# Folding the turn stage of a hybrid encoder block into its projection loop

## The chip, the cores and the metric

The kernel runs on one NeuronCore of one Trainium2 chip. The metric is the device time of one execution in microseconds (us), here the median of three runs. Profiles come from one further execution that the hardware profiler recorded.

## The reference: what is computed

Two groups of 256 tokens (512 in all, model width 1024) go through one encoder layer with the same weights. Cut to what matters here:

```
n1 = rmsnorm(h, W['norm_mix'][i])
proj = n1 @ W['w_in'][i]
xbc = silu(centred_depthwise_conv(xbc, conv_w) + conv_b)      # ssd: x, B, C
qkv = silu(centred_depthwise_conv(qkv, conv_w))               # gdn: q, k, v
q, k, v = l2norm(heads(q)), l2norm(heads(k)), heads(v)
```

After that come a bidirectional state-space scan over x, B and C (SSD), a bidirectional gated delta rule over queries, keys and values (GDN), a merge through an output projection, an expert layer (PEER) and a gated per-layer embedding. `l2norm` divides each head's 128 channels by the root of their sum of squares at each token. The scans want x, the values and also the keys by token and not by channel, so those are transposed.

## The kernel before, in words

The program is a row of stages with a barrier of all engines between them (`end_stage`). The change touches the first two. Five engines run side by side, each in the order of its own instruction list, and wait for one another by semaphores: TensorE (`pe`, in the profile PE), VectorE (`dve`), ScalarE (`act`), GpSimd (`pool`) and SyncE (`sp`), which issues the loads.

**`project_stage`** (L270 to L471). `NormT` (L201) squares the four token tiles of 128 tokens (ScalarE, L216), makes one root for all four (L229, L219, L231), scales them (VectorE, L233), transposes them into eight PSUM banks (TensorE, L245) and copies each bank out as a high part (ScalarE, L223) and a low part (VectorE, L237): `n_high` and `n_low`. A float32 product is made of three products of such parts (`products`, L172; L178, L179, L180). Then comes the small product with 64 columns (decays and gates), its transposes (L347), and a loop over 40 channel tiles: five trips of eight tiles (`Fori`). The order of the tiles in memory is x (8), B (4), C (4), queries (8), keys (8), values (8), by `CH_X` to `CH_V` (L475). For a tile TensorE runs 24 matmuls of 128x128 on 128x512. ScalarE takes the bank out with the centre tap (L405), VectorE adds three taps (L464), ScalarE applies silu (L400). Weights come in chunks of two tiles: SyncE loads 1 MB (L313), ScalarE makes the high part (L411), GpSimd the low part (L334). Behind the loop stand four small decay matmuls (L364), their exponential (L421) and a negation (L471).

**`turn_stage`** (L478 to L576) begins after the barrier. ScalarE squares the 16 tiles of queries and keys (L511). TensorE sums each over its 128 channels by a plain float32 matmul whose stationary operand is 128x16 (L529): tile k lands in row k of one bank. ScalarE takes the roots (L513), VectorE inverts them (L566), and high and low parts of the 16 rows are made (L517, L569). TensorE turns x and the values (L540), then spreads each inverse norm over 128 partitions with a 16x128 selector (L552, L553), VectorE multiplies (L575), and TensorE turns the keys. 24 groups of four transposes fill banks 4 to 7; ScalarE empties one half of them (L521), VectorE the other (L563).

**`ssd_stage`** (L644) begins after another barrier, with ScalarE at L675. It and all later stages keep their code, except that they find the tiles of B and C at other places of `channels`.

## Time and profile before

| what | us |
|---|---|
| median of 3 runs | 2458.65 (2453.87 to 2460.51) |
| the profiled execution | 2451.77 |
| its span, first to last instruction | 2450.0 |
| PE busy in the span | 2301.3 |
| DVE busy | 1529.1 |
| POOL busy | 1228.5 |
| ACT busy | 863.1 |

Busy time of PE is the union of its matmuls from start to modelled end. A matmul ends about 0.16 us after the next could start, so the pace of a row of matmuls is read from their starts. PEld is the load of the stationary operand, which overlaps PE. PEclk is TensorE's granted clock as a share of its full 2.4 GHz. L numbers are lines of the kernel before.

### The profile page before, as it was taken

The numbers are of one execution on the slowest core, as the hardware profiler recorded it, in microseconds if no ns is written. First come the engines' busy times: TensorE is split into PE (matmuls) and PEld (weight loads), VectorE is DVE, ScalarE is ACT, GpSimd is POOL, SyncE is SP. The second block draws the span as 40 slices with busy tenths as digits, with TensorE's granted clock in tenths as the row PEclk, the third lists the DMA queues.
The fourth block names the chain that finished last, engine by engine and source line by source line (L and its number), as shares of the span: only waits on it lengthen the run. The fifth ranks groups of instructions, "written<-read, shape, count | busy, mean of one in ns | idle before, by whom it ended". The sixth has DMA issues, their size and how long they took to land. (4 is left out here: it accounts for less than half of the span.)

```text
span 2450.0 us, 31801 instructions
## 1 busy us (share of the span) xinstructions
PE 2301.3 (94%) x10852; PEld 1890.1 (77%) x10852; DVE 1529.1 (62%) x3496; ACT 863.1 (35%) x1271; POOL 1228.5 (50%) x982
## 2 busy tenths in 40 slices
PE   7999889899979997989999999999989999999977
PEld 5888577788878886777888888888878888888865
DVE  5444488676764342119887887885238888888833
ACT  5443433334434331314333333333233233323322
POOL 3343086566544432413556656665647765555411
PEclk9999899999999998999999999999999999999989
DMA  4221011133344231314444444446449999999720
GB/s 144 101 88 66 0 57 39 41 120 128 129 145 173 93 117 41 128 36 144 141 142 141 141 141 142 142 142 210 142 146 405 378 377 361 356 349 349 299 103 35
DMA packets 158980, 393.98 MB, mean 161 GB/s; under 512 B 26304, under 2 KB 91968, under 8 KB 148160
## 3 DMA queue, kind: packets, MB, share of 16 engines
q1 hardware_dynamic: 124096, 325.79, 38.4%
q0 software_dynamic: 34816, 67.41, 7.4%
q8 instruction: 27, 0.44, 0.1%
q14 instruction: 41, 0.34, 0.0%
HBM read 327.92 MB, written 65.21 MB: 160 GB/s over the span
## 5 line engine op out<-in xcount | busy, mean ns | idle before, releaser
L1662 POOL DMA_INDIRECT g_dense<-up_gates_summed_sb,up_gate_at_sb x384 | 416.6, 1085 | 324.1 <-issue 230.3
L178 PE MATMUL ps<-n_high_sb,up_u_high_sb 128*128 128x512 f32 x1024 | 404.9, 395 | 7.9 <-DVE up_u_low_sb L1530 7.9
L179 PE MATMUL ps<-n_low_sb,up_u_high_sb 128*128 128x512 f32 x1024 | 404.5, 395 | 0.0
L180 PE MATMUL ps<-n_high_sb,up_u_low_sb 128*128 128x512 f32 x1024 | 404.5, 395 | 0.0
L1863 PE MATMUL ps<-down_v_high_sb,down_w_high_sb 128*128 128x512 f32 x768 | 299.6, 390 | 7.6 <-DVE down_w_low_sb L1813 7.6
L1864 PE MATMUL ps<-down_v_low_sb,down_w_high_sb 128*128 128x512 f32 x768 | 299.5, 390 | 0.0
L1865 PE MATMUL ps<-down_v_high_sb,down_w_low_sb 128*128 128x512 f32 x768 | 299.3, 390 | 0.0
L1530 DVE TENSOR_TENSOR up_u_low_sb<-up_u_sb,up_u_high_sb 128x1024 fp32r<-128x1024 f32 x128 | 156.5, 1223 | 173.7 <-ACT up_u_high_sb L1683 173.2
L1771 ACT ACTIVATE down_v_high_sb<-down_v_sb 128x1024 fp32r<-128x1024 f32 x128 | 134.3, 1049 | 322.8 <-PE ps L1865 289.5
L178 PEld LDWEIGHTS ps<-n_high_sb,up_u_high_sb 128*128 128x128 f32 x1024 | 193.3, 189 | 53.2 <-DVE up_u_low_sb L1530 8.1
L180 PEld LDWEIGHTS ps<-n_high_sb,up_u_low_sb 128*128 128x128 f32 x1024 | 193.3, 189 | 45.2
L179 PEld LDWEIGHTS ps<-n_low_sb,up_u_high_sb 128*128 128x128 f32 x1024 | 193.4, 189 | 45.0
L1696 ACT ACTIVATE up_gelu_sb<-ps 128x512 f32<-128x512 f32 x128 | 76.5, 597 | 418.3 <-PE ps L180 418.2
L1790 POOL DMA_INDIRECT expert_rows_sb<-expert_v,chosen_expert_sb x128 | 160.7, 1255 | 116.4 <-DVE h_sb L1829 63.3
L1811 DVE TENSOR_TENSOR down_v_low_sb<-down_v_sb,down_v_high_sb 128x1024 fp32r<-128x1024 f32 x128 | 156.4, 1222 | 71.2 <-ACT down_v_high_sb L1771 71.1
L1782 POOL DMA_INDIRECT down_picked_gelu_sb<-a_dense,chosen_gelu_at_sb x128 | 147.5, 1152 | 69.0 <-issue 69.0
L1863 PEld LDWEIGHTS ps<-down_v_high_sb,down_w_high_sb 128*128 128x128 f32 x768 | 144.6, 188 | 38.1 <-DVE down_v_low_sb L1811 8.1
L1171 POOL TENSOR_TENSOR merge_low_sb<-merge_slots_sb,merge_high_sb 128x2048 fp32r<-128x2048 f32 x19 | 88.2, 4640 | 167.8 <-ACT merge_high_sb L1159 167.8
L464 DVE SCALAR_TENSOR_TENSOR channels_sb<-ps,column_params_sb,channels_sb 128x510 f32 (+1 forms) x120 | 89.7, 748 | 126.5 <-ACT channels_sb L405 112.1
L1864 PEld LDWEIGHTS ps<-down_v_low_sb,down_w_high_sb 128*128 128x128 f32 x768 | 144.6, 188 | 30.1
L1865 PEld LDWEIGHTS ps<-down_v_high_sb,down_w_low_sb 128*128 128x128 f32 x768 | 144.6, 188 | 30.0
L334 POOL TENSOR_TENSOR w_low_sb<-w_slots_sb,w_high_sb 128x2048 fp32r<-128x2048 f32 x20 | 92.4, 4621 | 129.1 <-ACT w_high_sb L411 123.2
(324 smaller groups left out, 4729.7 us busy)
## 6 DMA issues: line engine op xcount, KB each, us to landing
up_u_sb<-expert_u SPq DMA_DIRECT2D x128, 512.0 KB, 3.8
down_v_sb<-expert_v SPq DMA_DIRECT2D x32, 2048.0 KB, 11.9
a_dense<-up_gelu_sb SPq DMA_DIRECT2D x128, 256.0 KB, 2.2
g_dense<-nought_sb SPq DMA_DIRECT2D x8, 3072.0 KB, 10.4
down_gelu_sb<-a_dense SPq DMA_DIRECT2D x32, 768.0 KB, 4.8
down_gates_sb<-g_dense SPq DMA_DIRECT2D x32, 768.0 KB, 6.5
w_slots_sb<-w_conv SPq DMA_DIRECT2D x20, 1024.0 KB, 4.9
query_slots_sb<-peer_query SPq DMA_DIRECT2D x8, 1024.0 KB, 5.3
```

The costliest lines, as they stand in the source:

```text
L178: pe.matmul(out, ah, bh, start=k == 0, stop=False)
L179: pe.matmul(out, ah, bl, start=False, stop=False)
L180: last = pe.matmul(out, al, bh, start=False, stop=k == n - 1)
L1530: dve.tensor_tensor(ul[:, n, :, :], u[:, n, :, :], bits32(uh[:, n, :, :]), ALU.subtract).then_inc(low, 1)
L1662: pool.indirect_dma_start(cells, at, summed[:, tt, k:k + 1], None).then_inc(stored[tt], 16)
L1771: act.activation(vh[b][:, j, :], v[:, b, j, :], ACT.Copy).then_inc(v_high, 1)
L1782: pool.indirect_dma_start(picked[:, u, k:k + 1], None, gelus, at).then_inc(gelu_in[n % 2], 16)
L1790: pool.indirect_dma_start(m.rows[:, s, :], None, experts, at).then_inc(row_in[s], 16)
L1811: dve.tensor_tensor(vl[b][:, j, :], v[:, b, j, :], bits32(vh[b][:, j, :]), ALU.subtract).then_inc(v_low, 1)
L1863: pe.matmul(m.ps[:, q, :], wh[:, b, j, t], vh[b][:, j, c], start=start, stop=False)
L1864: pe.matmul(m.ps[:, q, :], wh[:, b, j, t], vl[b][:, j, c], start=False, stop=False)
L1865: return pe.matmul(m.ps[:, q, :], wl[:, b, j, t], vh[b][:, j, c], start=False, stop=stop)
```

## The change

`turn_stage` is gone as a stage. Its work stands inside `project_stage`, whose loop over 40 tiles is written out. The tiles now come in the order x, keys, values, queries, B, C, and `laid` maps this to the unchanged order of the weights. Each tile product is followed on TensorE by what is due behind that tile: a sum over the squares of the tile two before (16 in all), a spread of one or two inverse norms (16 in all, of two matmuls each), and a group of four transposes (24 in all). Sums are kept for eight heads at a time, with a 128x128 stationary operand cut from `strip`, and the selectors of the spreads are 128x128 too. Tile products use banks 0 to 3 and no longer 0 to 7. The decay matmuls stand behind tile 19, the small product behind tile 1 and its transposes behind tile 2.

The norm becomes `NormTiles`: each token tile is squared, rooted, scaled and transposed by itself. SyncE loads only the first square (the identity) and the columns' parameters between the tokens; the other constants come later; the first weight chunk is loaded and split in two halves.

The core of the diff:

```diff
-    for stage in (project_stage, turn_stage, ssd_stage, gdn_stage, merge_stage):
+    for stage in (project_stage, ssd_stage, gdn_stage, merge_stage):
...
+CH_X, CH_K, CH_V, CH_Q, CH_B, CH_C = 0, 8, 16, 24, 32, 36
...
-    norm = NormT(nc, m, m.region(AT_CH, AT_WORK), "mix_norm", COL_MIX)
+    norm = NormTiles(nc, m, m.region(AT_CH, AT_WORK), "mix_norm", COL_MIX)
...
+    BANKS = 4
+    NH = GDN_H
+    SQUARED = 2
+    LAG = 2
+    FIRST = (CH_K, CH_Q)
+    NORMS_AT = [c + NH + LAG for c in FIRST]
+    SPREAD_AT = [t + 3 for t in NORMS_AT]
+    DECAYS_AT = NORMS_AT[0] + 1
...
+    def turns_behind(t):
+
+        for n, first in enumerate((CH_X + 6, CH_V + 6, CH_V + 14)):
+            if first <= t < first + 8:
+                return [8 * n + t - first]
+        return []
...
+    def spreads_behind(t):
+        if SPREAD_AT[0] <= t < SPREAD_AT[0] + NH:
+            return [t - SPREAD_AT[0]]
+        k = 2 * (t - SPREAD_AT[1])
+        return [NH + n for n in (k, k + 1) if 0 <= n < NH] if t < N_CONV else [NH + n for n in range(max(k, 0), NH)]
...
+            for t in range(N_CONV):
+                tile_product(t, first if t == 0 else lambda k: None)
+                if t == 1:
+                    pe.wait_ge(small_low, 1)
+                    products(pe, m.ps[0:64, 6, :], [(wsh[:, k, :], wsl[:, k, :]) for k in range(KT)],
+                             [(m.nh[:, k, :], m.nl[:, k, :]) for k in range(KT)]).then_inc(small_prod, 1)
...
+                k = head_of(t - LAG)
+                if k is not None:
...
+                    pe.wait_ge(squared, k + 1)
+                    j = k % NH
+                    pe.matmul(m.ps[:, 4, :], strip[:, NH - 1 - j:NH - 1 - j + P], s2[:, k % SQUARED, :], start=j == 0,
+                              stop=j == NH - 1).then_inc(summed, 1)
...
+                spreads(t)
+                for g in turns_behind(t):
+                    base, _, half, tt = turn(g)
+                    if base == CH_K:
+                        pe.wait_ge(scaled, 4 * half + 4)
+                    else:
+                        pe.wait_ge(active, base + 4 * half + 4)
+                    if g >= 2:
+                        pe.wait_ge(copied[g % 2], g // 2)
+                    for a in range(4):
+                        last = pe.transpose(m.ps[:, 6 + g % 2, a * P:(a + 1) * P],
+                                            m.ch[:, base + half * 4 + a, tt * P:(tt + 1) * P], sq(m, "eye"))
+                    last.then_inc(turned, 1)
+            spreads(N_CONV)
```

The turn stage before, on TensorE, from the last rows of the projection on (L364 the decays, L529 the sums, L540 the transposes, L552 and L553 the spreads):

```order
L180 MATMUL ps<-n_high_sb,w_low_sb 128x512
L350 REGISTER_ALU
L350 COMPARE_AND_BRANCH
L364 MATMUL ps<-decay_sb,squares_sb 128x64 x4
L299 UNCONDITIONAL_BRANCH
L523 UNCONDITIONAL_BRANCH
L529 MATMUL ps<-squares_of_sb,column_strip_sb 16x512 x16
L540 MATMUL ps<-squares_sb,channels_sb 128x128 x64
L552 MATMUL ps<-norms_high_sb,row_selectors_sb 128x512
L553 MATMUL ps<-norms_low_sb,row_selectors_sb 128x512
```

Sums, transposes and spreads stand there in blocks of their own, and no tile product is left to run between them.

TensorE in the changed kernel, behind the product of tile 26 (L513 a sum, L488 a spread, L532 a group of transposes):

```order
L180 MATMUL ps<-n_high_sb,w_low_sb 128x512
L513 MATMUL ps<-squares_of_sb,column_strip_sb 128x512
L488 MATMUL ps<-norms_high_sb,row_selectors_sb 128x512
L488 MATMUL ps<-norms_low_sb,row_selectors_sb 128x512
L532 MATMUL ps<-squares_sb,channels_sb 128x128 x4
L178 MATMUL ps<-n_high_sb,w_high_sb 128x512
```

One sum, one spread and one group have moved between two tile products. Tiles 26 to 28 carry all three kinds; from tile 6 to tile 37 all but tiles 18 to 20 carry at least one, and tile 19 carries the decays.

ScalarE in the changed kernel, around tile 34, where the second norm is made (L583 centre tap, L553 silu, L598 the root, L566 a transposed half, L541 a high part, L601 the high part of the norms):

```order
L583 ACTIVATE channels_sb<-ps,column_params_sb 128x512
L553 ACTIVATE channels_sb<-channels_sb 128x512
L598 ACT_TABLE_LOAD
L598 ACTIVATE norms_of_sb<-ps,eps_sb 128x512
L566 ACTIVATE channels_sb<-ps 128x512
L583 ACTIVATE channels_sb<-ps,column_params_sb 128x512
L541 ACTIVATE w_high_sb<-w_slots_sb 128x2048
L553 ACT_TABLE_LOAD
L553 ACTIVATE channels_sb<-channels_sb 128x512
L601 ACTIVATE norms_high_sb<-norms_of_sb 128x512
```

The root, which stood alone in the turn stage, now stands between two silus, and costs a table load before it and another behind it.

## Rows read from the trace of the kernel before

**Rows 1.** The page, part 1: busy time, share of the span, instructions.

```profile
PE 2301.3 (94%) x10852; PEld 1890.1 (77%) x10852; DVE 1529.1 (62%) x3496; ACT 863.1 (35%) x1271; POOL 1228.5 (50%) x982
```

**Rows 2.** Stretches: us, busy by engine, granted clock, DMA share, GB/s.

```profile
21.20:28.90 7.70, 6.18 (x28) 3.47 (x28) 4.86 (x8) 6.29 (x10) 4.22 (x2) 1.00 0.40 136
28.90:252.10 223.20, 223.18 (x960) 181.02 (x961) 97.18 (x138) 96.77 (x108) 85.21 (x19) 1.00 0.23 80
252.10:259.80 7.70, 1.00 (x9) 0.86 (x7) 2.47 (x4) 3.59 (x5) 0.00 (x0) 0.85 0.00 0
259.80:304.60 44.80, 40.90 (x160) 24.65 (x160) 22.11 (x30) 19.29 (x31) 2.04 (x3) 0.80 0.00 0
```

**Rows 3.** Groups by line, 28.9 to 252.1 us: busy, mean ns, idle before.

```profile
L334 POOL TENSOR_TENSOR w_low_sb<-w_slots_sb,w_high_sb 128x2048 fp32r<-128x2048 f32 x19 | 87.8, 4623 | 126.7 <-ACT w_high_sb L411 123.2 <-ACT w_high_sb L373 3.5
L464 DVE SCALAR_TENSOR_TENSOR channels_sb<-ps,column_params_sb,channels_sb 128x510 f32 (+1 forms) x117 | 87.5, 748 | 123.1 <-ACT channels_sb L405 109.1 <-DVE channels_sb L464 13.9
L411 ACT ACTIVATE w_high_sb<-w_slots_sb 128x2048 fp32r<-128x2048 f32 x18 | 34.3, 1905 | 0.0
```

**Rows 4.** Timeline of the start: start us, length us, instruction, idle before.

```profile
4.22 1.06 ACT L216 ACTIVATE mix_norm_scaled_sb<-h_sb 128x1024 f32<-128x1024 f32 x1 [2.20 <-DMA h_sb<-x_prompt]
9.77 1.28 ACT L219 ACT_TABLE_LOAD   x1
13.27 0.17 DVE L229 TENSOR_SCALAR stat_sb<-stat_sb 128x4 f32<-128x4 f32 x1 [13.27 <-DMA row_params_sb<-row_params]
14.83 5.48 PE L245 MATMUL ps<-squares_sb,mix_norm_scaled_sb 128*128 128x128 f32 x32 [14.83 <-DVE mix_norm_scaled_sb L233]
19.65 4.73 ACT L223 ACTIVATE n_high_sb<-ps,column_params_sb 128x512 fp32r<-128x512 f32 x8 [1.51 <-PE ps L245]
21.27 0.41 PE L178 MATMUL ps<-n_high_sb,w_small_high_sb 128*64 128x512 f32 x1 [0.96 <-DVE n_low_sb L237]
```

**Rows 5.** Timeline, end of the projection and start of the next two stages.

```profile
252.38 0.78 ACT L405 ACTIVATE channels_sb<-ps,column_params_sb 128x512 f32<-128x512 f32 x1 [4.29 <-PE ps L180]
255.26 0.75 DVE L464 SCALAR_TENSOR_TENSOR channels_sb<-ps,column_params_sb,channels_sb 128x510 f32 x1 [0.17 <-DVE channels_sb L464]
258.47 0.23 DVE L471 TENSOR_SCALAR gdn_neg_decay_sb<-gdn_decays_sb 128x128 f32<-128x128 f32 x1 [2.47 <-ACT gdn_decays_sb L421]
259.83 2.19 ACT L511 ACTIVATE squares_of_sb<-channels_sb 128x512 f32<-128x512 f32 x4 [1.39 <-PEq L198]
305.37 0.31 ACT L675 ACTIVATE decay_high_sb<-decay_sb 128x128 fp32r<-128x128 f32 x1 [1.32 <-PEq L198]
```

**Rows 6.** Prices of the moved work: a group by line, and the timeline.

```profile
L529 PE MATMUL ps<-squares_of_sb,column_strip_sb 128*16 128x512 f32 x32 | 15.7, 654 | 7.5 <-ACT squares_of_sb L511 7.5
L575 DVE SCALAR_TENSOR_TENSOR channels_sb<-channels_sb,ps 128x512 f32<-128x512 f32 x16 | 10.2, 684 | 0.8 <-PE ps L553 0.8
276.24 2.40 PE L540 MATMUL ps<-squares_sb,channels_sb 128*128 128x128 f32 x20
287.62 0.49 PE L552 MATMUL ps<-norms_high_sb,row_selectors_sb 16*128 16x512 f32 x1
287.95 0.38 PE L553 MATMUL ps<-norms_low_sb,row_selectors_sb 16*128 16x512 f32 x1
2397.35 7.03 PE L1934 MATMUL ps<-w_ple_proj_sb,p_t_sb 128*128 128x512 f32 x16
```

**Rows 7.** Stretches inside the turn stage, columns as in rows 2.

```profile
291.40:298.50 7.10, 7.10 (x18) 4.95 (x16) 6.44 (x11) 0.00 (x0) 0.00 (x0) 0.51 0.00 0
298.50:301.00 2.50, 2.50 (x13) 2.43 (x13) 1.13 (x3) 0.60 (x1) 0.00 (x0) 0.50 0.00 0
301.00:304.00 3.00, 2.85 (x22) 2.62 (x20) 1.76 (x4) 1.74 (x3) 0.00 (x0) 0.86 0.00 0
```

**Rows 8.** DMA queues, 28.9 to 252.1 us: packets, MB, share of 16 engines.

```profile
q8 instruction: 2, 0.03, 0.1%
q14 instruction: 2, 0.02, 0.0%
```

More of the change, by code:

```diff
@@ L287, in project_stage @@
+    norms_h, norms_l = (split_r.take(f"norms_{x}", [P, T], F32R) for x in ("high", "low"))
+    strip = split_r.take("column_strip", [P, NH - 1 + P])
+    rows = split_r.take("row_selectors", [P, NH, P], F32R)
     w_in = [m.sem(f"w_slot{j}_loaded") for j in range(2)]
+    part_in = [m.sem(f"w_first{h}_loaded") for h in range(2)]
+    part_high, part_low = m.sem("w_first_high_done"), m.sem("w_first_low_done")
     ws_in, small_high, small_low = m.sem("w_small_loaded"), m.sem("w_small_high"), m.sem("w_small_low")
@@ L360, in _, with tile_product @@
[L360 to L365 removed]
+            def tile_product(t, ready=lambda k: None):
+                j = (t // 2) % 2
+                f = slice((t % 2) * P, (t % 2 + 1) * P)
+                if t >= 2 and t % 2 == 0:
+                    pe.wait_ge(low, t // 2)
+                if t >= BANKS:
+                    pe.wait_ge(conv, t - BANKS + 1)
+                products(pe, m.ps[:, t % BANKS, :], [(wh[:, j, k, f], wl[:, j, k, f]) for k in range(KT)],
+                         [(m.nh[:, k, :], m.nl[:, k, :]) for k in range(KT)], ready).then_inc(prod, 1)
@@ new lines, in first, with spreads @@
+            def first(k):
+                pe.wait_ge(norm.out_done, k + 1)
+                if k % HALF == 0:
+                    pe.wait_ge(part_low, k // HALF + 1)
+            def spreads(t):
+                for n in spreads_behind(t):
+                    if n == 0:
+                        pe.wait_ge(made, 2)
+                        pe.wait_ge(act_small, 1)
+                    if n % NH == 0:
+                        pe.wait_ge(split_l, n // NH + 1)
+                    if n >= 1:
+                        pe.wait_ge(scaled, n if n <= NH else n - 1)
+                    for last, part in enumerate((norms_h, norms_l)):
+                        ins = pe.matmul(m.ps[:, spread_bank(n), :], rows[:, n % NH, :], part[:, :], start=last == 0, stop=last == 1)
+                    ins.then_inc(spread, 1)
@@ new lines, in silu, with copies @@
+            def silu(t):
+                ct = m.ch[:, t, :]
+                act.wait_ge(conv, t + 1)
+                act.activation(ct, ct, ACT.Silu).then_inc(active, 1)
+                k = head_of(t)
+                if k is not None:
+                    act.wait_ge(active, t + 1)
+                    if k >= SQUARED:
+                        act.wait_ge(summed, k - SQUARED + 1)
+                    act.activation(s2[:, k % SQUARED, :], ct, ACT.Square).then_inc(squared, 1)
+            def copies(t):
+                for g in turns_behind(t):
+                    if g % 2 == 0:
+                        _, out, half, tt = turn(g)
+                        act.wait_ge(turned, g + 1)
+                        act.activation(out[:, tt, half * CW:(half + 1) * CW], m.ps[:, 6, :], ACT.Copy).then_inc(copied[0], 1)
@@ new lines, in copies, with scale @@
+            def copies(t):
+                for g in turns_behind(t):
+                    if g % 2 == 1:
+                        _, out, half, tt = turn(g)
+                        dve.wait_ge(turned, g + 1)
+                        dve.tensor_copy(out[:, tt, half * CW:(half + 1) * CW], m.ps[:, 7, :]).then_inc(copied[1], 1)
+            def scale(n):
+                dve.wait_ge(spread, n + 1)
+                c = m.ch[:, FIRST[n // NH] + n % NH, :]
+                dve.scalar_tensor_tensor(c, c, 1.0 if n < NH else GDN_D ** -0.5, m.ps[:, spread_bank(n), :],
+                                         ALU.mult, ALU.mult).then_inc(scaled, 1)
```

473 lines of the change are left out of this document (236 added, 237 removed).

## The prediction

> **What bounds the kernel now.** I read the page's busy shares first: PE is busy 94% of the span [rows 1], so time is to be had where PE is idle, slow, or busy with work that could be cheaper. Then I cut the beginning into stages [rows 2]. Between 28.9 and 252.1 us PE runs the 40 tile products with no gap: 960 matmuls in 223.2 us, 0.2325 us each, 5.6 us a tile, at full clock. In this stretch the other engines wait for PE: VectorE and GpSimd each stand idle for more than 120 us before their main work [rows 3]. Then come 7.7 us with little PE work and the turn stage, 44.8 us long, where PE looks busy (40.9 us) but has a mean clock of 0.80. There are two stages with opposite limits: one where PE is the only bound, and one where ScalarE, VectorE and PE take turns. From the last work of the projection (258.7 us) to the last of the turn stage (304.6) it is 45.9 us, its barrier included; the SSD stage starts at 305.4 [rows 5]. Since everything behind that is unchanged and starts from a barrier, the whole question is when the SSD stage starts. A barrier costs 1.1 us between last work and first work at 259.8, and 0.8 us at 305.4.
>
> At the beginning, the vector work of the norm waits until 13.27 us for constants that it doesn't use, and the first copy out of PSUM waits for PE until 19.65 [rows 4].
>
> **Part 1, the start.** Now each token tile is rooted alone. ScalarE's squares begin at 4.22 us as before; four squares (1.06 us each and 0.2 us to read the sum), a table load of 1.28 and four roots of 0.2 take it to about 11.4. Before, it reached the table load at 9.77 and then waited. VectorE scales at 0.94 us a tile (four took 3.76 us) and 0.2 us for each reciprocal; the last starts behind root and third scaling at 12.7, and is done at 13.8. PE starts its transposes near 9.5 and not at 14.83, so 24 of the 32 are behind it by then; the 32 took 5.48 us. The first copy comes at about 14.4 where it came at 19.65. From that copy to the first matmul it was 1.6 us. I take 16.2 us for the first matmul of tile 0. The bounds are 14.5 (the transposes hide wholly) and 18.5 (the halved weights land late; before, a whole chunk was still being waited for at 16.2, with more bytes ahead of it). From there PE owes the small product, 24 matmuls at 0.23 or 5.6 us, which used to be followed by a wait: the loop began at 28.9 [rows 2]. Now the stream of tile products is in effect ahead by 28.9 - 16.2 - 5.6 = 7.1 us. The wait for the small results goes, since tile 2 runs meanwhile.
>
> **Part 2, what PE takes up.** All of it is on the path, because PE has no gap in this stretch.
> - 16 sums: each is a plain float32 matmul that the profile shows as two instructions. With 16 columns these kept a pace of 0.43 us at full clock (32 took 15.7 us [rows 6], the first few slower). For the full 128x128 shape the nearest row is L1934: 16 in 7.03 us, (7.03 - 0.16)/16 = 0.43. So full shape costs the same: 16 x 0.86 = 13.8 us.
> - Spreads: 12 of the 16 stand ahead of the end of the last product; 24 matmuls x 0.23 = 5.5 us.
> - 96 transposes: 20 in 2.40 us, less the last one's tail of 0.27, gives 0.11 each [rows 6]; 10.6 us.
> - Going back from transposes to a 512-column matmul: the first spread is 0.33 us ahead of the second, where 0.23 is the pace. So 0.1 us for each of 24 groups, 2.4 us. The bounds are nothing (sums and spreads may need none) and 0.2 us at each of some 55 places where the kind changes, 11 us.
> - Small transposes 0.5 us and decays 0.7 us, which stood outside the stream before: 1.2.
>
> The last product then ends at 16.2 + 223.2 + 5.6 + 13.8 + 5.5 + 10.6 + 2.4 + 1.2 = 278.5 us.
>
> **Part 3, what lies beside it.** A tile with inserts lasts about 6.5 us. VectorE per tile: three taps, 2.8 us with their gaps, at most 1.4 for two scalings and 0.7 for a copy. ScalarE: 0.78 centre tap, 0.62 silu, 0.63 square, 0.6 for every second group, 1.9 for a high part every second tile [rows 3, 5]; a reload pair adds 2.6 us four times. GpSimd: 4.6 us per two tiles [rows 3], and its selector copy about 1. All lie under PE's time. The 3.3 us reciprocals (the same 512 columns, though now 128 rows) each make one tile's taps late by about 2 us, and four banks let PE run three tiles ahead. I cost all this at nothing. If that cover were gone, each late tile would cost what the chain lacks, as in the first rival. The tightest chain is the sum: the square of tile t stands on ScalarE behind the centre tap and silu of the next tile's turn, 0.2 + 0.78 + 1.9 + 0.62 + 0.63 = 4.1 us after product t+1, and PE asks for it 5.6 us after. Behind that wait, in PE's order, stand all later products. The loads have more room than that: SyncE is released by GpSimd as before.
>
> **Part 4, the end.** From the last product VectorE's taps end 3.9 us later (252.1 to 256.0 [rows 5]). Then four scalings of 0.68 and a spread between them: 7.0 us in all. Before, the end was at 258.7, 6.6 us behind. So 278.5 + 7.0 = 285.5, and with 0.8 for the barrier the SSD stage starts at 286.3 instead of 305.4.
>
> **Sum:** 45.9 (the stage and its barrier) + 7.1 (start) - 33.5 (part 2) - 0.4 (end) = 19.1 us, and 305.4 - 286.3 is the same. The profiled execution would go from 2451.8 to 2432.7. It is 6.9 us under the median of the runs shown; against the median I say 2458.65 - 19.1 = 2439.5.
>
> **A rule against it.** Transposes are now strewn over the stream. The rows show what transposes alone do to the clock: it stood at 0.50 (1.2 GHz) when they began at 298.5 and was back up within the next stretch, 0.86 on average, while PE ran nothing else [rows 7]. The Trainium skill, "TensorE: Matmul & The Clock Gate", Part 4: PE-mode transpose, says that transpose mode doesn't count as PE being busy and that the full clock doesn't engage for it. By it the 96 transposes would run at half clock; this trace disagrees. In numbers from rows that would add 96 x 0.11 = 10.6 us, and the median would be 2450.
>
> **Rivals.**
> *Small stalls at every tile (10%).* PE waits at each of the 16 sums, because ScalarE runs later than worked out, or the written-out code isn't fetched in time. At 1 us each 16 us go: 2455.5. Against it: a margin of 1.5 us, and idle times of over 100 us on the side engines [rows 3]. As to fetching, four instruction packets arrived in the loop stretch [rows 8] while PE was busy for 223.18 of 223.20 us.
> The Trainium skill, "Runtime: NRT & Kernel Launch", Instruction fetch mechanics, says that straight code streams mostly hidden and that a taken branch can stall; a gap at the old loop's turns is not seen in rows 2.
> *The clock falls (6%), slower than before.* Inserts of another kind bring TensorE to 1.2 GHz inside the stream. It did so once: after some 4 us of spreads with a 16-row selector the clock was 0.51 for 7.1 us, with PE never idle [rows 7]. At half clock a tile's 24 matmuls take 0.43 each and not 0.23, 4.7 us more. Four such tiles eat the 19.1 us; from six on it is slower beyond the bound. If every one of the eight tiles with a single spread ran so it would be 37.6 us, and 2477. Against: a spread is now 0.46 us among more than 5 us of full products, and has 128 rows.
> *The change doesn't do what it says at the start (4%).* The halved weights land as late as the chunk did; PE starts tile 0 at 21 us. That costs 5: 2444.5.
> *All works as forecast (80%).* 2439.5, from 2433 (start 14.5, no cost for returning to products, and small savings: 19.1 + 1.7 + 2.4 + 2) to 2450 (start 18.5, and 0.2 us at each change of kind: 19.1 - 2.3 - 8.6).
>
> **Numbers.** The range is the forecast's own, with a little of the stalls: 2432 to 2451. A measurement of this kernel can tell about 0.3%, 7.4 us, from no change. Faster by more: forecast, late start, and a few cases of the stalls, 0.86. Within: most of the stalls, 0.08. Slower: the clock, 0.06.
>
> **What would show it.** In the changed profile: the first matmul of tile 0 near 16 us; starts of L178 rows 5.6 us apart in a bare tile and 6.0 to 7.4 in filled ones; L513 at 0.43 per instruction; PE with hardly an idle time before L513, L488 and L532; clock 1.00 from 20 us to the last product at 278; the SSD stage's first work at 286; and the same lengths behind it. I would be wrong if L513 shows idle times released by ScalarE's squares, if the clock column falls under 0.95 in the stream, or if PE's busy time in the stretch is higher than the sum of part 2 allows.

## The result, and the profile after

| | before | changed | |
|---|---|---|---|
| median of 4 runs, us | 2456.86 | 2436.99 | ratio 0.9919, 95% interval 0.9905 to 0.9934 |
| the profiled execution, us | 2451.77 | 2437.48 | |
| its span, us | 2450.0 | 2435.7 | |
| SSD stage's first work, us | 305.37 | 284.24 | 21.1 earlier |
| GDN stage's first work, us | 450.32 | 431.71 | 18.6 earlier |

The changed kernel is 19.9 us faster by the medians. Page, part 1, of the changed kernel:

```profile
PE 2303.4 (95%) x10852; PEld 1895.0 (78%) x10852; DVE 1537.4 (63%) x3504; ACT 861.6 (35%) x1275; POOL 1219.3 (50%) x983
```

PE is as busy as before [rows 1], in a span that is 14.3 us shorter. Stretches of the changed kernel (columns as in rows 2): the stream from tile 0 to tile 39, the end of the stage, and the start of the SSD stage.

```profile
16.70:276.30 259.60, 259.60 (x1148) 204.68 (x1148) 132.85 (x174) 121.42 (x150) 90.25 (x22) 1.00 0.22 74
276.30:283.10 6.80, 3.25 (x10) 1.73 (x8) 4.74 (x7) 1.93 (x3) 0.00 (x0) 0.82 0.00 0
284.20:289.20 5.00, 2.17 (x5) 1.82 (x6) 0.35 (x2) 3.38 (x8) 3.80 (x4) 0.50 0.36 107
```

The first line answers to the second of rows 2: PE has no idle time in 259.6 us, at full clock, with all the inserts in it. Behind it the clock falls: 0.82, then 0.50. The groups by line in that stretch:

```profile
L178 PE MATMUL ps<-n_high_sb,w_high_sb 128*128 128x512 f32 x320 | 130.2, 407 | 0.9 <-DVE n_low_sb L297 0.9
L456 POOL TENSOR_TENSOR w_low_sb<-w_slots_sb,w_high_sb 128x2048 fp32r<-128x2048 f32 x19 | 87.9, 4626 | 146.4 <-ACT w_high_sb L541 146.4
L679 DVE SCALAR_TENSOR_TENSOR channels_sb<-ps,column_params_sb,channels_sb 128x510 f32<-128x510 f32 (+1 forms) x117 | 87.1, 747 | 118.3 <-ACT channels_sb L583 115.4
L513 PE MATMUL ps<-squares_of_sb,column_strip_sb 128*128 128x512 f32 x32 | 16.3, 591 | 0.0
L532 PE MATMUL ps<-squares_sb,channels_sb 128*128 128x128 f32 x96 | 14.4, 272 | 0.0
L488 PE MATMUL ps<-norms_high_sb,row_selectors_sb 128*128 128x512 f32 x12 | 5.9, 493 | 0.0
```

The last number of the sums (L513), transposes (L532) and spreads (L488) is the idle time of PE before them: 0.0. The 0.9 us beside L178 is a wait for the norm's low parts that ends at 16.42, ahead of the first product of tile 0 and so ahead of the stretch. The side engines still wait for more than 110 us, as in rows 3. The start, on the timeline of the changed kernel:

```profile
9.31 6.17 PE L245 MATMUL ps<-squares_sb,mix_norm_scaled_sb 128*128 128x128 f32 x32 [9.31 <-DVE mix_norm_scaled_sb L286]
12.04 1.06 ACT L547 ACTIVATE w_high_sb<-w_slots_sb 128x1024 fp32r<-128x1024 f32 x1 [0.32 <-DMA w_slots_sb<-w_conv]
14.82 3.01 ACT L273 ACTIVATE n_high_sb<-ps,column_params_sb 128x512 fp32r<-128x512 f32 x5 [1.72 <-PE ps L245]
16.42 0.50 PE L178 MATMUL ps<-n_high_sb,w_high_sb 128*128 128x512 f32 x1 [0.94 <-DVE n_low_sb L297]
```

PE's transposes start 5.5 us earlier than in rows 4 and ScalarE's first copy out 4.8 us earlier. The end of the stage and the start of the next:

```profile
277.53 2.32 DVE L679 SCALAR_TENSOR_TENSOR channels_sb<-ps,column_params_sb,channels_sb 128x508 f32<-128x508 f32 x3 [2.99 <-ACT channels_sb L583]
280.49 0.67 PE L488 MATMUL ps<-norms_high_sb,row_selectors_sb 128*128 128x512 f32 x1 [2.89 <-DVE channels_sb L650]
280.96 0.63 PE L488 MATMUL ps<-norms_low_sb,row_selectors_sb 128*128 128x512 f32 x1
282.48 0.69 DVE L650 SCALAR_TENSOR_TENSOR channels_sb<-channels_sb,ps 128x512 f32<-128x512 f32 x1 [0.17 <-PE ps L488]
284.24 0.31 ACT L786 ACTIVATE decay_high_sb<-decay_sb 128x128 fp32r<-128x128 f32 x1 [3.73 <-PEq L198]
```

**Two balances.** From stage to stage: 21.1 us won up to the SSD stage's start. In this pair of profiles the SSD stage is 2.5 us longer (147.5 and 144.9 us), and the code behind it, which is the same, 4.3 us longer (2435.7 - 431.7 = 2004.0 and 2450.0 - 450.3 = 1999.7). That leaves 14.3, the difference of the spans. Over the 14 profiles of this study the code behind the SSD stage lasted 1999.5 to 2007.7 us: 1999.5 to 2004.3 in the three with a turn stage, 2000.2 to 2007.7 in the eleven with the folded one. The ranges overlap, and whether the 4.3 us have to do with the change is not shown. The profile of before is a quick one, 5.1 us under its own median. The experiments are read by the length of the stream (first to last product) and the start of the SSD stage first, and by medians second.

### The profile page after: what moved, and what is told of

It reads as the page before. It is cut to its first block and busy times, and to the rows that moved or that the text cites. A ratio compares the mean times of both kernels' runs of the same rounds, so it can differ in the third digit from the quotient of the medians.

```text
span 2435.7 us, 31180 instructions
## 1 busy us (share of the span) xinstructions
PE 2303.4 (95%) x10852; PEld 1895.0 (78%) x10852; DVE 1537.4 (63%) x3504; ACT 861.6 (35%) x1275; POOL 1219.3 (50%) x983
## 5 line engine op out<-in xcount | busy, mean ns | idle before, releaser
L178 PE MATMUL ps<-n_high_sb,up_u_high_sb 128*128 128x512 f32 x1024 | 404.9, 395 | 8.3 <-DVE up_u_low_sb L1641 8.0
L178 PEld LDWEIGHTS ps<-n_high_sb,up_u_high_sb 128*128 128x128 f32 x1024 | 193.5, 189 | 53.6 <-DVE up_u_low_sb L1641 8.1
L1975 PEld LDWEIGHTS ps<-down_v_low_sb,down_w_high_sb 128*128 128x128 f32 x768 | 144.9, 189 | 30.1
L679 DVE SCALAR_TENSOR_TENSOR channels_sb<-ps,column_params_sb,channels_sb 128x510 f32<-128x510 f32 (+1 forms) x120 | 89.3, 747 | 121.4 <-ACT channels_sb L583 118.4
L456 POOL TENSOR_TENSOR w_low_sb<-w_slots_sb,w_high_sb 128x2048 fp32r<-128x2048 f32 x19 | 87.9, 4626 | 146.4 <-ACT w_high_sb L541 146.4
```

The source lines that it names most:

```text
L178: pe.matmul(out, ah, bh, start=k == 0, stop=False)
L1975: pe.matmul(m.ps[:, q, :], wh[:, b, j, t], vl[b][:, j, c], start=False, stop=False)
```

## The experiments

In every run "first" is the start of the first matmul of tile 0, "last" that of the last L178, and "SSD" the first work of the SSD stage.

| run | first | last | SSD | median (runs) | ratio to before, 95% interval |
|---|---|---|---|---|---|
| before, profiled | 28.9 | 251.4 | 305.4 | | |
| changed | 16.4 | 275.8 | 284.2 | 2436.99 (4) | 0.9919 (0.9905 to 0.9934) |
| changed, again | 16.5 | 275.9 | 284.2 | 2435.13 (7) | 0.9911 (0.9879 to 0.9943) |
| old start | 21.7 | 281.2 | 289.6 | 2445.59 (12) | 0.9944 (0.9923 to 0.9966) |
| new start only | 23.9 | 247.9 | 302.9 | 2450.54 (12) | 0.9978 (0.9956 to 0.9999) |
| full shapes in turn stage | 29.3 | 254.2 | 304.3 | 2452.57 (12) | 0.9990 (0.9962 to 1.0017) |
| transposes twice | 15.6 | 285.7 | 293.4 | 2447.36 (10) | 0.9958 (0.9942 to 0.9974) |
| narrow shapes | 16.8 | 283.6 | 292.1 | 2443.50 (6) | 0.9949 (0.9928 to 0.9970) |
| narrow spreads alone | 16.8 | 279.8 | 288.1 | 2441.91 (4) | 0.9945 (0.9924 to 0.9967) |
| sums of one part | 15.5 | 264.8 | 272.6 | 2431.90 (4) | 0.9898 (0.9870 to 0.9926) |
| last spreads early | 16.0 | 276.3 | 282.6 | 2435.50 (4) | 0.9902 (0.9871 to 0.9933) |
| one part and early | 15.7 | 266.0 | 272.3 | 2427.22 (4) | 0.9878 (0.9854 to 0.9902) |
| idle filled | 16.5 | 275.9 | 283.7 | 2437.01 (5) | 0.9915 (0.9901 to 0.9928) |
| both and filled | 16.0 | 266.2 | 272.5 | 2429.79 (4) | 0.9878 (0.9863 to 0.9894) |

**The changed kernel once more**, with no edit.

> The changed kernel once more, as the partner of the next three. If the gain is made wholly ahead of the SSD stage, ScalarE's first work there (L786) starts at 284.2 us again, 21.1 us earlier than before, and the time is 19 to 22 us under that of the kernel before. If the later stages really gave back the 6.9 us by which the first profile's remainder was longer (2151.5 against 2144.6 us), then this profile's remainder is again near 2151 and the gain near 15 us; if that was chance, the remainder lies anywhere in 2144 to 2152.

The stage starts repeat within 0.1 us here, the median is 20.3 us under that of before. From the start of the SSD stage to the end the profile shows 2151.6 us, again near 2151.5 and above the 2144.6 of before, the sign that was named for something being given back; the gain of 15 us that should go with it is not what the medians show. The later runs with the same code up to tile 0 put their first matmul anywhere from 15.5 to 16.8 us, so the start scatters by more than this pair shows; the stream's length, 259.4 us in both, is the steadier figure.

**The old start in the changed kernel.** One part of the change is taken back:

```diff
-    norm = NormTiles(nc, m, m.region(AT_CH, AT_WORK), "mix_norm", COL_MIX)
+    norm = NormT(nc, m, m.region(AT_CH, AT_WORK), "mix_norm", COL_MIX)
```

with the constants loaded ahead of the weights, as before.

> The changed kernel with the old norm (one root for four tiles) and the old order of the loads. Theory, PE alone bounds the stream: the first matmul of tile 0 moves from 16.4 to about 21.3 us (where the first product stood before), and the SSD stage's start from 284.2 by the same 4.9 us to 289.1; time 4.9 us over the changed kernel. Rival, the later start is absorbed by slack in the stream or the loads: the SSD stage starts at less than 286.

The first matmul comes 5.3 us later, and that carries through the whole stream: last product 5.3 later, SSD stage 5.4 later. So PE is the bound from end to end. By the medians the cost is 10.5 us, though the intervals of the two ratios overlap. That is more than the stage shows; in the profile 3.5 us of it sit behind the SSD stage (2007.5 us there against 2004.0), and the rest stays open.

**The new start in the kernel before**, the reverse of it.

> The kernel before with nothing but the new norm and the new order of loads (the first weight chunk stays whole; turn stage, loop and barriers stay). Theory: the first copy out of PSUM comes at 14.8 instead of 19.65 us and everything behind it is 4.8 us earlier, the SSD stage starts at 300.6 instead of 305.4, and the gain is 4.8 us of the 21.1. Then 16.3 us belong to the dissolved stage. Rival: a later wait (weights, 24.2 us second high part) takes over, and the gain is under 2 us.

The loop starts 5.0 us earlier, but the SSD stage in this profile only 2.5. The timeline of this run, behind the small product, and then the same place in the kernel before:

```profile
22.66 0.46 PE L402 MATMUL ps<-squares_sb,small_t_sb 64*128 64x64 f32 x4 [0.68 <-ACT small_t_sb L440]
23.89 0.63 PE L178 MATMUL ps<-n_high_sb,w_high_sb 128*128 128x512 f32 x1 [0.77 <-ACT small_sb L442]
24.32 0.63 PE L179 MATMUL ps<-n_low_sb,w_high_sb 128*128 128x512 f32 x1
27.64 0.40 PE L178 MATMUL ps<-n_high_sb,w_high_sb 128*128 128x512 f32 x1
```

```profile
27.66 0.46 PE L347 MATMUL ps<-squares_sb,small_t_sb 64*128 64x64 f32 x4 [0.68 <-ACT small_t_sb L384]
28.92 0.49 PE L178 MATMUL ps<-n_high_sb,w_high_sb 128*128 128x512 f32 x1 [0.80 <-ACT small_sb L386]
```

PE waits twice for the small results (0.68 and 0.77 us), then runs 8 matmuls at 0.43 us and not 0.23: granted clock at its lower level, 1.2 GHz, 1.6 us lost. But the kernel before has the same two waits (0.68 and 0.80 us) and its clock read 1.00 up to the end of the loop, while the next run, whose start is that of before, fell to 1.2 GHz from 30.7 to 34.1 us. So this loss comes with these waits in some executions and not in others, and does not belong to the new start. Another 1.0 us lies in the turn stage, 55.0 us from the last product to the SSD stage where it was 54.0. By the medians, against the kernel before measured beside it (2455.47), the new start alone gains 4.9 us, which is what was expected. In the changed kernel the waits are covered by tile 2, and no profile of it shows a lower clock there. That the two halves of the change support one another, 2.5 us alone and 5.4 together, rests on single profiles with this scatter in them and is not shown.

**Full 128x128 shapes in the old turn stage**, with nothing else changed.

```diff
-    rows = work.take("row_selectors", [NQK, NQK, P], F32R)
+    rows = work.take("row_selectors", [P, NQK, P], F32R)
...
-                pe.matmul(m.ps[0:NQK, 0, :], strip[:, NQK - 1 - k:2 * NQK - 1 - k], s2[:, k % SLOTS, :], start=k == 0,
+                pe.matmul(m.ps[:, 0, :], strip[:, NQK - 1 - k:NQK - 1 - k + P], s2[:, k % SLOTS, :], start=k == 0,
```

> The kernel before with sums and spreads of its turn stage in the full 128x128 shape, all else the same. If it was the 16-row selectors that brought TensorE from 2.4 to 1.2 GHz at 291.4, the clock now stays at 1.00 through the spreads, matmuls keep 0.23 us, VectorE's scalings (0.64 us each) set the pace, and the turn stage is 2 to 4 us shorter (44.8 to about 42). Rival, the clock falls for another reason (time spent outside products, the small share of the work): it falls again at the same place and the stage keeps its 44.8 us.

The stretches of the turn stage with the spreads, of the kernel before and then of this run:

```profile
280.00:290.00 10.00, 9.00 (x54) 8.39 (x55) 7.86 (x13) 3.50 (x6) 0.00 (x0) 0.83 0.01 2
290.00:300.00 10.00, 10.00 (x30) 7.22 (x29) 8.54 (x14) 0.27 (x1) 0.00 (x0) 0.58 0.00 0
```

```profile
280.00:290.00 10.00, 7.47 (x65) 6.79 (x64) 8.27 (x9) 5.24 (x10) 0.00 (x0) 1.00 0.01 2
290.00:300.00 10.00, 10.00 (x47) 6.50 (x45) 9.82 (x18) 1.04 (x2) 0.00 (x0) 1.00 0.00 0
```

The lower clock in rows 7 came with the 16-row selectors. In both profiles that have them it fell among the spreads (at 291.6 us in the kernel before, at 286.9 in the run with the new start only); in the one with full selectors it stays at 1.00. The spreads last 8.8 us where they lasted 11.0 and 11.3, and what follows them, which in the kernel before began at the lower clock, 5.5 us where it was 6.8: 3.5 us together.

From the last product to the SSD stage it is 50.1 us where it was 54.0. Not all of that is the selectors': the 0.83 of the kernel before from 280 to 290 us is a fall to 1.2 GHz from 281.4 to 284.8, among transposes and ahead of the first spread at 287.62, which neither other profile with a turn stage has. The start and loop were 2.8 us slower in this profile (granted clock 0.83 from 30 to 40 us), and the median gains 2.9 us with an interval that holds 1. In the old layout the shapes are worth some 3.5 us of a stage by one profile, and a gain in time is not shown.

**Every transpose group twice**, to price what stands in the stream.

```diff
-                    for a in range(4):
+                    for a in [0, 1, 2, 3] * 2:
```

> The changed kernel with each of its 24 groups of four transposes issued twice into the same bank, so that nothing in the result changes. Theory, PE has no gap and everything it takes up is on the path: 96 more transposes of 0.09 us, the SSD stage starts 8.6 us later (292.8), the time is 8.6 us longer. Rival, part of the inserts hides in the pipeline of PE: less than half of that, under 4 us.

The stream from first to last product grows from 259.4 to 270.0 us, 10.6 us for 96 more transposes, still with no idle time on PE: all of it is on the path. That is 0.11 us each, where 0.09 was expected. The SSD stage starts only 9.2 us later, since the start was 0.8 us earlier and the last four spreads ran at full clock this time. Timeline of this run, one group of eight; then the changed kernel's group of four:

```profile
60.89 1.03 PE L532 MATMUL ps<-squares_sb,channels_sb 128*128 128x128 f32 x8
61.68 0.48 PE L178 MATMUL ps<-n_high_sb,w_high_sb 128*128 128x512 f32 x1
```

```profile
61.67 0.60 PE L532 MATMUL ps<-squares_sb,channels_sb 128*128 128x128 f32 x4
62.03 0.48 PE L178 MATMUL ps<-n_high_sb,w_high_sb 128*128 128x512 f32 x1
62.34 0.39 PE L179 MATMUL ps<-n_low_sb,w_high_sb 128*128 128x512 f32 x1
```

Four cost 0.36 us from start to start, eight 0.79: the second four cost 0.43, 0.11 each. Behind a group the first matmul takes 0.31 where 0.23 is the pace. A group of four with its return costs 0.36 + 0.08 = 0.44 us, the same as the second four, which bring no return of their own. The prediction had 0.54.

**Narrow sums and spreads in the stream.** The new order is kept, the shapes are those of the kernel before (8 columns for a sum, 8 rows for a selector).

```diff
-    rows = split_r.take("row_selectors", [P, NH, P], F32R)
+    rows = split_r.take("row_selectors", [NH, NH, P], F32R)
...
-                    pe.matmul(m.ps[:, 4, :], strip[:, NH - 1 - j:NH - 1 - j + P], s2[:, k % SQUARED, :], start=j == 0,
+                    pe.matmul(m.ps[0:NH, 4, :], strip[:, NH - 1 - j:NH - 1 - j + NH], s2[:, k % SQUARED, :], start=j == 0,
```

> The changed kernel with sums of 128x8 stationary operands and spreads with 8-row selectors, norms of 8 rows, all at the same places. Theory: a matmul's pace goes by its 512 columns, and a narrow matmul among full products doesn't bring the clock down; SSD start 284.2, same time within 1 us. Rival, that the full shapes are what keeps the clock: it falls under 1.00 between 150 and 190 us and 255 and 277 us, each tile at half clock costs 4.7 us, 284 becomes 290 or more.

Both theories fell. The clock reads 1.00 throughout the stream, and yet the SSD stage starts 7.9 us later: the stream has grown from 259.4 to 266.8 us. The next run shows where.

**Narrow spreads alone**, the sums left in full shape.

> The changed kernel with the spreads alone in their narrow form (selectors of 8 rows), the sums kept in full 128 by 128 form. Theory (each passage between a full and a narrow shape keeps the weight load from being pulled ahead and costs 0.1 us of the stream): in the run with both narrow the stream from first to last product grew by 266.8 - 259.4 = 7.4 us. There were 16 sums and 12 places with spreads among the tiles, 28 inserts, two passages each: 7.4 / 56 = 0.13 us a passage. With the spreads alone narrow 12 inserts are left, 24 passages: +3.2 us by the mean, +2.4 us by the 0.1 us read at a spread; the last product starts 262.0 to 262.6 us after the first, the SSD stage starts at 286.6 to 287.4 us, and the rows at the sums read as in the changed kernel (0.23 us behind the product, 0.86 us the pair). The rival (the cost of the narrow form lies in the sums' 8 columns, not in the passage): the stream stays at 259.4 us and the SSD stage starts at 284.2 us. The rival of the clock: the selectors of 8 rows bring the granted clock below 1.00 in the last windows before 283 us, and the SSD stage starts later than 288 us.

The stream is 263.0 us long, 3.6 more than in the changed kernel and a little above the 262.0 to 262.6 expected; the clock again stays at 1.00 up to 280 us. Timeline of this run around the first spread, matmuls and then weight loads:

```profile
156.82 0.40 PE L180 MATMUL ps<-n_high_sb,w_low_sb 128*128 128x512 f32 x1
157.15 0.49 PE L488 MATMUL ps<-norms_high_sb,row_selectors_sb 8*128 8x512 f32 x1
157.49 0.39 PE L488 MATMUL ps<-norms_low_sb,row_selectors_sb 8*128 8x512 f32 x1
157.81 0.50 PE L178 MATMUL ps<-n_high_sb,w_high_sb 128*128 128x512 f32 x1
158.15 0.39 PE L179 MATMUL ps<-n_low_sb,w_high_sb 128*128 128x512 f32 x1
```

```profile
157.15 0.18 PEld L488 LDWEIGHTS ps<-norms_high_sb,row_selectors_sb 8*128 8x128 f32 x1 [0.37 <-issue]
157.25 0.18 PEld L488 LDWEIGHTS ps<-norms_low_sb,row_selectors_sb 8*128 8x128 f32 x1
157.81 0.19 PEld L178 LDWEIGHTS ps<-n_high_sb,w_high_sb 128*128 128x128 f32 x1 [0.36 <-issue]
```

And a spread of the changed kernel, matmuls and weight loads:

```profile
162.48 0.39 PE L180 MATMUL ps<-n_high_sb,w_low_sb 128*128 128x512 f32 x1
162.71 0.39 PE L488 MATMUL ps<-norms_high_sb,row_selectors_sb 128*128 128x512 f32 x1
162.94 0.40 PE L488 MATMUL ps<-norms_low_sb,row_selectors_sb 128*128 128x512 f32 x1
```

```profile
162.48 0.19 PEld L488 LDWEIGHTS ps<-norms_high_sb,row_selectors_sb 128*128 128x128 f32 x1
162.71 0.19 PEld L488 LDWEIGHTS ps<-norms_low_sb,row_selectors_sb 128*128 128x128 f32 x1
```

With full shapes the weights of the spread are loaded from 162.48 on, while the product before it starts: one matmul ahead, and the pace stays 0.23. With a narrow selector the load begins only at 157.15, together with its own matmul, and the full load behind it is held up in the same way at 157.81. The steps are 0.33, 0.34, 0.32 and 0.34 us where the pace is 0.23: 0.10, 0.11, 0.09 and 0.11 us more, 0.4 for this place. Where transposes follow the spread instead of a product it is 0.35. The 12 spreads stand at 10 places, since two places hold a pair that shares the way in and out (the expectation counted 12 places). These 10 places, at 0.34 to 0.41 us, make the 3.6 us by which the stream grew; step by step, the two profiles agree everywhere else. The other 3.8 us of the run with both narrow are the 16 sums, 0.24 us each on average. What the full shapes are worth here is therefore 7.4 us of stream, by keeping the weight loads ahead, and not the clock.

Not every change of shape does this. In the changed kernel itself the small product, whose stationary operand is 128x64, stands between tile 1 and tile 2. Matmuls, then a weight load:

```profile
27.46 0.39 PE L180 MATMUL ps<-n_high_sb,w_low_sb 128*128 128x512 f32 x1
27.68 0.40 PE L178 MATMUL ps<-n_high_sb,w_small_high_sb 128*64 128x512 f32 x1
```

```profile
27.46 0.13 PEld L178 LDWEIGHTS ps<-n_high_sb,w_small_high_sb 128*64 128x64 f32 x1
```

Its load is one matmul ahead and nothing is lost, nor on the way out (matmuls at 32.96, 33.19 and 33.42 us). So the load was late for 8 rows of 128 columns (the spreads) and for 128 rows of 8 columns (the sums), and not for 128 rows of 64 columns. Which property decides stays open.

The Trainium skill, "TensorE: Matmul & The Clock Gate", Step-by-step: what each phase is for, says that a weight load is pulled ahead of running matmuls when the row groups don't conflict or when it goes to the background buffer. By it nothing speaks against a pull-ahead into the background in any shape. The rows agree for equal shapes and for the step between 128 and 64 columns, and show that between the full shape and 8 rows or 8 columns it did not happen here in either direction. The same page, LDWEIGHTS (loading the stationary operand), says that the load takes its time by columns and not by rows; 0.18 us with 8 rows and 0.19 with 128 agree, and so does 0.13 with 64 columns.

**Sums of one part.** The squares are rounded once to the form that a product's high part has, and summed by one instruction and not two; the low parts of the squares are left out of the norms, which are a little less exact for it.

```diff
-    s2 = split_r.take("squares_of", [P, SQUARED, T])
+    s2 = split_r.take("squares_of", [P, SQUARED, T], F32R)
...
```

> The changed kernel with the squares rounded to the high-part format and summed by one matmul of 0.23 us each instead of a plain float32 one of 0.86 us. The squares' low parts are left out, so the norms are a little less exact. Theory: 16 x 0.63 = 10.1 us less on PE and on the path, SSD start at 274.1. Rival, one of the side engines is near its limit (ScalarE's chain of 4.1 us against 5.6): waits appear before the sums, and less than 7 us are gained.

The group of the sums in this run, over the stream:

```profile
L516 PE MATMUL ps<-squares_of_sb,column_strip_sb 128*128 128x512 f32 x16 | 6.3, 395 | 0.0
```

The stream is 249.4 us long, 10.0 less, and 16 x (0.86 - 0.23) = 10.1. The sums' term is confirmed to a tenth. The SSD stage starts 11.6 us earlier; an earlier start (1.0) and last spreads at full clock (0.6) make the rest.

**The last key scalings three tiles earlier.** The spreads 12 and 13 move behind tile 38 into banks 6 and 7, the spreads 14 and 15 behind tile 39, so that no spread waits for a scaling at the end.

```diff
-        k = 2 * (t - SPREAD_AT[1])
-        return [NH + n for n in (k, k + 1) if 0 <= n < NH] if t < N_CONV else [NH + n for n in range(max(k, 0), NH)]
+        return {SPREAD_AT[1]: [8, 9], SPREAD_AT[1] + 1: [10, 11, 12, 13], SPREAD_AT[1] + 2: [14, 15]}.get(t, [])
...
```

> The changed kernel with the last six spreads moved ahead (four behind tile 38, two of them in the banks of the transposes, two behind tile 39), so that only two scalings are left behind the last taps. Theory: the last product ends 0.9 us later, because four matmuls more stand ahead of it; the end behind it takes 5.2 instead of 6.9 us; SSD start 0.8 us earlier, 283.4. Rival: VectorE's four scalings ahead of the last taps make those late, and nothing is gained or 1 us lost.

From the last L178 to the SSD stage it is 6.3 us and not 8.4, for 0.9 us more of stream; net 1.2 us. The median cannot tell that.

**Both of these together**, the fastest version by the median. Like the run with short sums it leaves the squares' low parts out of the norms.

> The changed kernel with the sums of the squares' high parts alone (as in the run with sums of one part; the low parts of the squares are left out of the norms) and the last key scalings done three tiles earlier (as in the run with the early spreads). If both savings lie on the same path, one behind the other, they add: 19.9 us of the stream and start were won by the changed kernel, 10.7 us more by the short sums (272.6 against 284.2, less 0.9 of an earlier start), 1.2 us more by the early spreads. The SSD stage would start at 284.2 - 10.7 - 1.2 = 272.3 us (271.4 if the start is again 0.9 us earlier), and the time by the medians is 2431.9 - 1.2 = 2430.7 us, range 2425 to 2434. The rival: something else than TensorE ends the last stage when the stream is 10 us shorter (ScalarE's casts of the weights at 35% busy, GpSimd's subtractions, or VectorE's taps of the last tile), so that idle time before L178 appears and the start of the SSD stage stays at 273 us or later.

The stream of this run:

```profile
16.00:266.80 250.80, 250.80 (x1137) 202.62 (x1136) 133.97 (x176) 121.35 (x150) 90.99 (x22) 1.00 0.23 77
```

The savings add: the SSD stage starts at 272.3 us, with PE still never idle. It runs in 2427.22 us, ratio 0.9878 (0.9854 to 0.9902) to before.

**The idle time filled.** Products that nobody reads stand in PE's wait before the last two spreads (11) and at the start of the SSD stage (10).

```diff
...
+            for n in range(10):
+                pe.matmul(bank(0, 2), m.nh[:, 0, 0:P], m.nh[:, 0, :], start=True, stop=True)
             pe.wait_ge(split_high, 2)
```

> The changed kernel with matmuls whose result nobody reads in the two idle stretches of TensorE around the stage's end: 11 full 128 by 128 products in the 2.89 us before the last two spreads, and 10 at the start of the SSD stage, where it waits for ScalarE. It tests what the lower granted clock costs there, and whether it is what the SSD stage gives back (147.5 us long against 144.9 before, granted clock 0.50 in its first 5 us against 0.83). Theory: it is. Then the clock reads 1.00 from 276 to 292 us, the four halves of the last spreads start 0.23 us apart instead of 0.43 (the SSD stage starts 0.6 us earlier, at 283.6 us), the first scores of the SSD stage take about half of 3.77 us, its first running sum (L852 in the changed kernel) starts at 289.5 us instead of 290.25 where GpSimd's decay steps then end the wait, and the stage is 145 to 146 us long: SSD stage end 2 to 3 us earlier than in the changed kernel, time by medians 2433 to 2434 us. The rival: the SSD stage's length is set by GpSimd and VectorE (DVE busy 9.8 of 10 us in the stretch 10 us after its start), the filled start leaves it at 147 us or more, and the time stays within 1 us of the changed kernel's. Against both: filler that lasts longer than the wait and pushes the spreads back; then the SSD stage starts later than 284.2 us.

Timeline of this run at the start of the SSD stage, then a row of the changed kernel:

```profile
284.51 4.11 PE L834 MATMUL ps<-n_high_sb 128*128 128x512 f32 x10 [2.57 <-PEq L198]
288.46 1.89 PE L841 MATMUL ps<-channels_sb,b_stage_sb 128*128 x8
```

```profile
287.03 3.77 PE L835 MATMUL ps<-channels_sb,b_stage_sb 128*128 x8 [4.59 <-ACT b_stage_sb L795]
```

The part before the last spreads did what it should: the SSD stage starts 0.5 us earlier. The part in the SSD stage did not: the filler itself ran slowly at first (4.11 us for ten, which is 2.3 at full clock) and pushed the scores back by 1.8 us after GpSimd and ScalarE had made them ready. Most of that came back only because they then took half the time; the first running sum starts at 290.00 us where it started at 290.25. The clock is up from 288.0 on, and the stage is 148.4 us long, where it was 147.5 and 145 to 146 were expected. The same filler in the faster version:

> The run with short sums and early spreads (SSD stage start 272.3 us, median 2427.2 us), with the 10 unread products at the start of the SSD stage as in the other run of this pair. If the lower clock at that start costs what the theory says, the stage's first 8 us go 0.7 us faster, and what follows 1 to 2 us more: 2425 us by the medians, range 2421 to 2428. The rival (GpSimd and VectorE set the stage's length): the SSD stage is as long as in the run without the filler, within 0.5 us, and the time is 2427 us.

Stage length 147.6 us as without it (147.55), median 2429.79 against 2427.22, with the same ratio to before (0.9878). So the lower clock in the first microseconds of the SSD stage is not what makes it long. What does stays open: it lasted 144.9 us in before, 146.1 and 146.4 in the two other kernels with a turn stage, 146.4 to 148.4 in the eleven profiles with the folded stage. The mean granted clock over the whole stage goes the same way: 0.99 in before, 0.96 in the two others with a turn stage, 0.94 or 0.95 with the folded one. Whether the clock makes the stage long, or what makes it long also lowers the clock, is not shown. Some 1 us may belong to the change.

## Why the prediction was right

A sum in the changed kernel, for the prices below, on its timeline between a product and four transposes:

```profile
85.76 1.02 PE L513 MATMUL ps<-squares_of_sb,column_strip_sb 128*128 128x512 f32 x2
86.62 0.60 PE L532 MATMUL ps<-squares_sb,channels_sb 128*128 128x128 f32 x4
```

- **The path.** "The other engines wait for PE" held. PE had no idle time in 259.6 us, and each edit of PE's work (10.6 us of transposes more, 10.0 us of sums less) came out in the length of the stream in full, as the 5.3 us of the old start did at its end.
- **The start**, 16.2 us forecast, 16.42 measured; ScalarE's first copy at 14.82 for the forecast 14.4. The rival in which the halved weights are late (21 us) didn't occur: the second half was cast at 12.04.
- **The sums**, 13.8 us forecast from L1934: 85.76 to 86.62 is 0.86 us, 16 of them 13.8. **The spreads**, 0.23 us an instruction: as forecast, and nothing extra on entering either.
- **Transposes and the return to products**, 10.6 + 2.4 = 13.0 us forecast, 24 x 0.44 = 10.6 measured. This is the one mis-sized term of any weight: the return was charged on top of four transposes at 0.11 us each, and it is already in them. The 0.1 us for it was read from 287.62 and 287.95 in rows 6, two spreads with a narrow selector. The run with full shapes in the turn stage has nearly the same step at that place:

```profile
290.09 0.48 PE L552 MATMUL ps<-norms_high_sb,row_selectors_sb 128*128 128x512 f32 x1
290.41 0.39 PE L553 MATMUL ps<-norms_low_sb,row_selectors_sb 128*128 128x512 f32 x1
```

So the long step is there with full shapes as well, but the matmul ahead of it then follows the last transpose closely. In the stream a group costs 0.36 up to that matmul and 0.08 behind it, 4 x 0.11 in all, and a return of its own costs nothing.
- **The end of the stream**: 278.5 forecast, 276.5 measured. What comes behind it: 6.7 us to VectorE's last scaling for the forecast 7.0, then 1.1 us of barrier for 0.8. SSD stage: 286.3 forecast, 284.2 measured; start +0.2, transposes with their return -2.4, small transposes and decays +0.3 (0.6 and 0.9 us for the 1.2 forecast), end -0.3 and barrier +0.3 make -1.9, and rounding is the rest.
- **The beside work** cost nothing, as said: the reciprocals (3.35 us each) and a constant's scaling of 4.49 us on VectorE (L636) made no idle time on PE.
- **"The same lengths behind it"** is not shown: 2.5 us more in the SSD stage in this pair and 4.3 behind it. Against the kernel before measured beside them, the medians of the eleven runs with the folded stage gain 3.0 us less on average than the start of their SSD stage (from 1.0 more to 8.5 less); those of the two other runs with a turn stage gain about 2 more. So part of what is won may be given back later, and why stays open. That the time came nearer to the forecast (19.9 us for 19.1) than the stage start did (21.1) is luck: the stage started 2 us earlier than forecast, and some of that was lost again behind it.
- **The rival of the clock** did not occur, but its reason was half right: in both profiles in which 32 matmuls with 16-row selectors ran back to back the clock fell to 1.2 GHz among them (0.51 in rows 7), and with full ones it stayed at 1.00. Spread among full products, even 8-row ones did not.
- **The rule against it.** 96 transposes among the products left the clock at 1.00 and cost 0.11 us each, the way back included. The Trainium skill, "TensorE: Matmul & The Clock Gate", Part 4: PE-mode transpose, would have them at half clock; by it the stream would have been 10.6 us longer, and the trace disagrees.
- **The code written out.** q8, which brings instructions, delivered more than in rows 8, and no idle time came of it:

```profile
q8 instruction: 9, 0.15, 0.2%
```

The old order left 45.9 us to a stage in which PE, ScalarE and VectorE took turns; PE's part of that is 33.5 us forecast, some 31 measured, and the rest was waiting and low clock. That difference, some 15 us, is what folding the stage gave, and the start gave the rest: 5.4 us by the run with the old start.

## What to carry to other kernels

Where one engine bounds a long stretch without a gap and a later stage has several engines taking turns, move the later stage's work into the stretch: it costs the bounding engine's own time and no more, so price exactly that, instruction by instruction. On TensorE give what is inserted the shape of what surrounds it, even if most rows or columns are zero: a full 128x128 operand cost nothing here beyond its 0.23 us, while a sum with 8 columns cost 0.24 us more and a place with spreads of 8 rows 0.34 to 0.41. An operand with 64 columns cost nothing more either, so not every padding pays. Read a price from a row whose neighbours have the shapes of the new place, and over the whole insert from start to start: one long step can be made up by a short one beside it.

## What was not expected of the hardware

- Between a full 128x128 stationary operand and one of 8 rows or 8 columns the weight load did not run ahead. For a spread that cost 0.09 to 0.11 us at each step in and out, and as much once more in the step behind each (0.33, 0.34, 0.32, 0.34 us where 0.23 is the pace). A third narrow matmul in a row is back at 0.24 (280.92 to 281.16 us in the run with narrow spreads). Between 128 and 64 columns nothing was lost.
- The same short waits can cost clock or not. After 0.68 and 0.77 us of idle time around four small transposes 8 matmuls ran at 0.43 us (1.2 GHz) in one profile; with the same waits a like stretch began 1.4 us behind them in another, and none in the kernel before. After 2.89 us of idle time four spreads ran at 0.43 us each in the changed kernel, and at full clock after 2.88 and 2.90 us in the runs with doubled transposes and with short sums. Filling that idle time with 11 unread products brought 0.5 us in one profile, and filling a wait that others end brought nothing.
- Stretches in which PE is never idle repeat to 0.1 us (259.4 us in the changed kernel, its repeat, the run with the old start and the one with the idle time filled). The start scattered by 1.3 us, and the 2000 us of identical code behind the SSD stage by up to 8 us. A change in the first tenth of a kernel is better read from the stretch that it touches and from the start of the next stage than from one time. What the later stages make of it needs medians.
